# A recurrence's steps spread over a round of weight pieces, and an output projection whose last row blocks come after two columns

## The reference, cut to what matters

```python
def rglru(x, w_a, b_a, w_x, b_x, lam, reverse):
    r = sigmoid(einsum('bshc,hce->bshe', xh, w_a) + b_a)
    i = sigmoid(einsum('bshc,hce->bshe', xh, w_x) + b_x)
    log_a = -LRU_C * softplus(-lam) * r
    a = exp(log_a)
    u = sqrt(-expm1(2.0 * log_a)) * (i * x)
    _, h = lax.associative_scan(_recurrence_combine, (a, u), reverse=reverse, axis=1)
    return h

def recurrent_group(xr, gr, ...):
    xc = centred_depthwise_conv(xr, conv_w, conv_b)
    h = rglru(xc, ..., reverse=False) + rglru(xc, ..., reverse=True)
    return gelu(gr) * h
...
h = h + concatenate([a_out, b_out], axis=-1) @ w_out      # a_out: the recurrence, b_out: the gating
h = h + peer(rms_norm(h, ffn_norm_g), ...)
```

## Time and profile before

| | us |
|---|---|
| median of 3 runs | 3032.75 (3028.52 to 3043.32) |
| the profiled execution | 3043.12 |
| its span, first to last instruction | 3041.8 |
| TensorE busy in the span | 2912.6 (96%) |
| input projection of the second mixer in the span | 1254.3 to 1434.7 |
| second output projection | 1434.7 to 1528.5 |

### The profile page before, as it was taken

The page is one execution under the profiler, slowest core; times in us unless marked ns, Lnnn a source line. Parts: engine busy times, 40 slices in busy tenths (PEclk is TensorE's granted clock), DMA queues, the critical chain, the costliest instruction groups (busy, mean ns, idle before and its releaser), DMA issues.

```text
span 3041.8 us, 45087 instructions
## 1 busy us (share of the span) xinstructions
PE 2912.6 (96%) x18238; PEld 2622.7 (86%) x18238; DVE 2178.8 (72%) x3236; ACT 1594.5 (52%) x2418; POOL 412.5 (14%) x311
## 2 busy tenths in 40 slices
PE   7999989999999998988998899999999999999998
PEld 6888777888888886988888799999999999999997
DVE  5455457777776445554579899877999877999776
ACT  4477745555554444566444455544555544556543
POOL 0011100111111000242121000033110033100130
PEclk9999999999999999999999899999999999999999
DMA  6534354555555553633654455688766688666784
GB/s 239 180 139 141 136 194 146 186 184 189 183 191 215 193 192 139 223 138 133 222 181 153 168 192 181 224 313 314 246 234 232 222 317 314 237 231 228 279 308 165
DMA packets 99150, 631.42 MB, mean 208 GB/s; under 512 B 11520, under 2 KB 12928, under 8 KB 31360
## 3 DMA queue, kind: packets, MB, share of 16 engines
q1 hardware_dynamic: 80512, 561.43, 52.3%
q0 software_dynamic: 18432, 67.12, 6.1%
HBM read 623.26 MB, written 4.19 MB: 206 GB/s over the span
## 4 chain that ended last, share of the span: by engine, by line
PE 62%; DVE 10%; DMA 10%; ACT 3%; issue 1%; POOL 1%; ACTq 0%; DVEq 0%; POOLq 0%
PE ps L277 24%; PE ps L278 12%; PE ps L1260 5%; DMA ring<-in_u_rows_dram,idx 5%; DMA ring<-in_v_rows_dram,idx 5%; PE ps L299 4%; PE ps L300 4%; PE ps L301 4%; DVE loR L259 3%; PE ps L1262 3%; DVE ring L1321 1%; PE ps L1171 1%; PE ps L288 1%; PE ps L289 1%; PE ps L290 1%
## 5 line engine op out<-in xcount | busy, mean ns | idle before, releaser
L259 DVE TENSOR_TENSOR loR<-raw,hiR 128x1024 fp32r<-128x1024 f32 x1007 | 1266.1, 1264 | 600.8 <-ACT hiR L251 593.4
L251 ACT CAST hiR<-raw 128x1024 fp32r<-128x1024 f32 x1026 | 1073.7, 1049 | 715.1 <-PE ps L1262 320.2
L277 PE MATMUL ps<-XA,hiR 128*128 128x448 f32 (+1 forms) x3936 | 1355.5, 394 | 22.5 <-DVE S__142 L1203 22.0
L278 PE MATMUL ps<-XA,loR 128*128 128x224 f32 (+1 forms) x3936 | 1073.0, 273 | 0.0
L277 PEld LDWEIGHTS ps<-XA,hiR 128*128 128x128 f32 x3936 | 743.6, 189 | 140.5 <-DVE S__142 L1203 24.2
L278 PEld LDWEIGHTS ps<-XA,loR 128*128 128x128 f32 x3936 | 752.0, 191 | 2.5 <-issue 1.9
L1260 PE MATMUL ps<-hl,hiR 128*128 128x448 f32 x2048 | 648.8, 376 | 3.4 <-DVE loR L259 3.4
L1262 PE MATMUL ps<-hl,loR 128*128 128x224 f32 x2048 | 542.7, 265 | 0.0
L1260 PEld LDWEIGHTS ps<-hl,hiR 128*128 128x128 f32 x2048 | 384.4, 188 | 38.8 <-DVE loR L259 5.3
L1262 PEld LDWEIGHTS ps<-hl,loR 128*128 128x128 f32 x2048 | 391.4, 191 | 0.2 <-issue 0.2
L1299 POOL DMA_INDIRECT ring<-in_u_rows_dram,idx x64 | 103.2, 1613 | 727.8 <-DVE ring L1321 666.4
(11 more groups left out here) (284 smaller groups left out, 3473.1 us busy)
## 6 DMA issues: line engine op xcount, KB each, us to landing
raw<-in_u_dram SPq DMA_DIRECT2D x128, 1024.0 KB, 4.9
raw<-in_v_dram SPq DMA_DIRECT2D x128, 1024.0 KB, 5.7
raw<-in_w_up_dram SPq DMA_DIRECT2D x86, 1024.0 KB, 4.9
raw<-in_w_down_dram SPq DMA_DIRECT2D x43, 1024.0 KB, 4.9
raw<-in_w_in_qk_dram SPq DMA_DIRECT2D x32, 1024.0 KB, 4.9
raw<-in_w_out_dram SPq DMA_DIRECT2D x32, 1024.0 KB, 4.9
raw<-in_w_in_dram SPq DMA_DIRECT2D x24, 1024.0 KB, 4.9
raw<-in_w_in_v_dram SPq DMA_DIRECT2D x16, 1024.0 KB, 5.0
```

The costliest lines, as they stand in the source:

```text
L251: e.copy(hiR[:, r:r + 2, :], raw[n % NR][:, q:q + 2, :]).then_inc(S("hi"), 1)
L259: e.tensor_tensor(loR[:, r:r + 2, :], raw[n % NR][:, q:q + 2, :], hiR[:, r:r + 2, :].bitcast(F32), ALU.subtract).then_inc(S("lo_pool" if p ...
L277: e.matmul(both, wh, X.hl[:, :, k, 0:nt], start=(k == 0), stop=False, skip_group_check=True)
L278: m = e.matmul(dst[:, 0:nt], wl, X.h[:, k, 0:nt], start=False, stop=(k == KC - 1), skip_group_check=True)
```

## The change

Three things.

1. The chain of a round is spread over d = 25 to 42 in place of 23 to 32. Sigmoids: group 0 at 25, group 1 at 27. Tanh 29, gelu of `grT` 30, exp 31, square root 33. VectorE: 34, 35, and the scans at 36 and 38. Pool: products at 26 and 28, sums at 37 and 39, low parts at 40 and 42. High parts on ScalarE at 39 and 41. No operation is added or taken away.
2. In the input projection the pool makes no low parts any more; VectorE makes those eight pairs too.
3. The second output projection goes through columns 0 and 1 without row blocks 6 and 7, then (0, 6), (0, 7), (1, 6), (1, 7), then columns 2 and 3 as before. Column 0 is complete after 30 pieces and column 1 after 32 (before: 16 and 32), and `dve_x2` and the squares follow. The weights lie in HBM in the new order. SP's wait ahead of the four constant loads is for `gm_lo` and for `l_lo`, the recurrence's last low part.

```diff
-WO2_ORDER = [0, 1, 2, 3, 4, 5, 8, 9, 10, 11, 12, 13, 14, 15, 6, 7]
+MIX2 = [0, 1, 2, 3, 4, 5, 8, 9, 10, 11, 12, 13, 14, 15]
+WO2_ORDER = ([(0, k) for k in MIX2] + [(1, k) for k in MIX2] + [(0, 6), (0, 7), (1, 6), (1, 7)] +
+             [(2, k) for k in MIX2 + [6, 7]] + [(3, k) for k in MIX2 + [6, 7]])
+WO2_END = [30, 32, 48, 64]
...
-    if P_IN <= g < P_WO2:
-        return u % 6 == 0
...
-            if d == 23:
-                for i in range(2):
-                    c = 2 * p + i
...
-            elif d == 24:
+            if d in (25, 27):
+                i = (d - 25) // 2
+                c = 2 * p + i
...
+            elif d == 29:
...
-            if n % 16 == 0 and n:
-                dve_x2(e, n // 16 - 1)
+            if n in WO2_END:
+                dve_x2(e, WO2_END.index(n))
...
                 e.wait_ge(S("gm_lo"), 8)
+                e.wait_ge(S("l_lo"), 8)
```

More of the change, by code:

```diff
@@ L795, in act_mixer @@
             d = s - 24 * p
-            if d == 23:
-                for i in range(2):
-                    c = 2 * p + i
[L799 to L807, removed]
-            elif d == 24:
+            if d in (25, 27):
+                i = (d - 25) // 2
+                c = 2 * p + i
+                e.wait_ge(S("gates"), c + 1)
+                if p:
+                    e.wait_ge(S("hsum"), c - 1)
+                for v in range(2):
+                    e.activation(lR[i][:, v, :], bank[4 + 2 * i][:, v * T:(v + 1) * T], ACT.Sigmoid,
+                                 bias=lv[:, 40 + 8 * v + c:41 + 8 * v + c]).then_inc(S("sig"), 1)
+                for v in range(2):
+                    e.activation(lI[i][:, v, :], bank[5 + 2 * i][:, v * T:(v + 1) * T], ACT.Sigmoid,
+                                 bias=lv[:, 56 + 8 * v + c:57 + 8 * v + c]).then_inc(S("sig"), 1)
+            elif d == 29:
                 e.wait_ge(S("lam"), 24)
@@ L815, in act_mixer @@
                                      scale=lz[:, 80 + 8 * v + c:81 + 8 * v + c]).then_inc(S("tanh"), 1)
-            elif d == 25:
+            elif d == 30:
+                for i in range(2):
+                    c = 2 * p + i
+                    e.wait_ge(S("inev"), 6 * p + 2 + 2 * i)
+                    e.activation(grT[:, c, :], grT[:, c, :], ACT.Gelu_apprx_tanh).then_inc(S("grg"), 1)
+            elif d == 31:
                 for i in range(2):
@@ L823, in act_mixer @@
                                      scale=st[:, 200 + 8 * v + c:201 + 8 * v + c]).then_inc(S("aexp"), 1)
-            elif d == 26:
+            elif d == 33:
                 for i in range(2):
@@ L828, in act_mixer @@
                     e.activation(lR[i][:, :, :], lT[i][:, :, :], ACT.Sqrt, scale=-1.0).then_inc(S("lroot"), 1)
[L829 to L835, removed]
+            elif d in (39, 41):
+                c = 2 * p + (d - 39) // 2
                 e.wait_ge(S("hprod"), c + 1)
@@ L856, in dve_mixer @@
                                            lX[i][:, :], ALU.mult, ALU.add).then_inc(S("xc"), 1)
-            elif d == 26:
+            elif d == 34:
                 for i in range(2):
@@ L861, in dve_mixer @@
                                            ALU.mult).then_inc(S("q1"), 1)
-            elif d == 27:
+            elif d == 35:
                 for i in range(2):
@@ L866, in dve_mixer @@
                     e.tensor_tensor(lI[i][:, :, :], lI[i][:, :, :], lR[i][:, :, :], ALU.mult).then_inc(S("lu"), 1)
-            elif d in (28, 29):
-                i = d - 28
+            elif d in (36, 38):
+                i = (d - 36) // 2
                 e.wait_ge(S("lu"), 2 * p + i + 1)
@@ L888, in pool_mixer @@
             d = s - 24 * p
[L889 to L895, removed]
+            if d in (26, 28):
+                i = (d - 26) // 2
+                e.wait_ge(S("sig"), 8 * p + 4 * i + 4)
+                e.tensor_tensor(lI[i][:, :, :], lI[i][:, :, :], lX[i][:, None, :].to_broadcast([128, 2, T]),
+                                ALU.mult).then_inc(S("ix"), 1)
+            elif d in (37, 39):
+                i, c = (d - 37) // 2, 2 * p + (d - 37) // 2
                 e.wait_ge(S("scan"), 2 * c + 2)
@@ L900, in pool_mixer @@
                 e.tensor_tensor(lQ[i][:, 0, :], lQ[i][:, 0, :], grT[:, c, :], ALU.mult).then_inc(S("hprod"), 1)
-            elif d in (31, 32):
-                c = 2 * p + d - 31
+            elif d in (40, 42):
+                c = 2 * p + (d - 40) // 2
                 e.wait_ge(S("l_hi"), c + 1)
@@ L1464, in pe_program @@
                 pe_mixer(e, 4 * j + q)
-        for fb in range(4):
+        for n, (fb, k) in enumerate(WO2_ORDER):
             pair = (2 * (fb % 2), 2 * (fb % 2) + 1)
-            if fb == 0:
+            if n == 0:
                 e.wait_ge(S("inev"), 24)
-            elif fb >= 2:
+            elif (fb, k) == (1, 0):
+                e.wait_ge(S("gm_add"), 8)
+            elif fb >= 2 and k == 0:
                 e.wait_ge(S("x2"), 2 * (fb - 1))
[L1471 to L1478, removed]
+            e.wait_ge(S("l_lo" if k < 8 else "gm_lo"), k % 8 + 1)
+            moving(e, P_WO2 + n, XA.h[:, k, :], XA.l[:, k, :], [bank[b][:, :] for b in pair], k == 0, k == 7)
+            pe_mixer(e, 96 + n)
         for q in range(4):
@@ L1593, in act_program @@
             act_mixer(e, 96 + n)
-            if n % 16 == 1 and n > 16:
-                act_x2_square(e, n // 16 - 1)
+            if n - 1 in WO2_END:
+                act_x2_square(e, WO2_END.index(n - 1))
         act_x2_square(e, 3)
@@ L1754, in dve_x2 @@
     def dve_x2(e, fb):
-        e.wait_ge(S("piece"), P_WO2 + 16 * fb + 16)
+        e.wait_ge(S("piece"), P_WO2 + WO2_END[fb])
         for tb in range(2):
@@ L1965 @@
     a["w_in2"] = _stat(np.concatenate(blocks, 1))
-    a["w_out2"] = _mov(I["w_out_2"][0], [(fb, k) for fb in range(4) for k in WO2_ORDER])
+    a["w_out2"] = _mov(I["w_out_2"][0], WO2_ORDER)
     a["w_q"] = _stat(I["peer_w_q_2"][0])
```

## The result

| | us |
|---|---|
| before, median of 22 runs | 3037.99 (3028.52 to 3051.64) |
| changed, median of 22 runs | 3023.58 (3012.15 to 3037.67) |
| ratio | 0.9942, 95% interval 0.9930 to 0.9954 |
| profiled span | 3020.7 (before: 3041.8) |

A forecast was written before the change was run, and what follows sets the result against it. TensorE's single waits and the low clock behind them were taken to bound the kernel. The terms 11.3 + 4.4 + 3.6 - 1.0 - 0.5 = 17.8 us gave 3015 from the median 3032.75; range 3005 to 3029.

The forecast's parts named there:

- What bounds the kernel: Input and output projection: TensorE loses time in single waits and the low clock behind them, together 29 us.
- the ten waits: Input projection, rounds 1 to 3: TensorE waits for low parts from VectorE and the pool, costing 18.3 us, 6.1 a round.
- The walk: Step-by-step timing of one spread round from piece 24: waits at pieces 38, 40, 44 and 46, 2.35 us a round.
- The low clock: Input projection: four stretches at 1.2 GHz cost 5.8 us; one was expected to stay, so 4.4 us won.
- Rival (c): Input projection: spread waits keep TensorE at the low clock for long; with 20 such pieces 3044 us; chance 0.04.
- The border: Between the projections: `guT` comes ahead of the sigmoids, winning 3.6 us, 2.2 of wait and 1.4 of low clock.
- The output projection: Beside the last chain, early waits at pieces 14, 16 and 20 grow to about 2.5 from 1.5 us: -1.0 us.
- tile 8 and `x2`: Output projection, piece 32: tile 8 queued behind constant loads delays `x2`; none to 1.8 us of wait, taken as -0.5 us.
- The rest of the program is the same instructions in the same order: Outside the changed stages: claimed nothing differs, so no gain or loss was counted there.
- The rule of the shared port: VectorE with two SBUF inputs and the pool: the first takes the ports, the other blocks; a 1.22 us subtraction took 3.42.
- Rival (d): ScalarE's chain: a table switch costs 1.4 us more than its load, 5.5 us more wait a round; about 3037; chance 0.02.
- Rival (a): Both projections: stalls only move, all four low-clock stretches remain; 9.3 us won, 3023.5 us; chance 0.33.

The follow-up runs named there:

- part 2 alone: The kernel before with no low parts on the pool in the input projection, chain not spread: 173.4, 90.5 and 12.8 us; ratio to before 0.9964.

## Why the prediction was right, and where not

**What bounds the kernel** held, and so did the reading of the ten waits as 18.3 us. By this count the wait of the walk's check, at piece 30, is 0.91 + 0.16 = 1.07 us; the 1.19 in the text runs from the start of the matmul before. **The walk** named the three pieces that wait in every round. Its sizes were 0.55, 1.2 and 0.45 (with 0.15 at piece 46), 2.35 us a round; the trace has 0.63, 0.66 and 1.34, 2.63 us. The 1.2 was too large because the two products took 1.29 us together and not 1.75; the 1.8 of the earlier trace rows has a blocked part in it. The 0.45 was too small by the pool: I took 2.1 us for sum and product from the earlier trace rows, and they took 3.25, since VectorE's subtraction now stands right ahead of the sum. So the 11.3 of the sum is 10.4.

**The low clock** was 4.4 us of the sum, on the reading that one of four stretches stays. None did: 5.8 us. With the 10.4 that makes 16.2, and with the 2.4 at the border 18.6 for the stage. Rival (c), the low clock for longer, has nothing in this stage; but whether the clock falls can't be read from a single wait: the wait of 2.3 us at piece 32 brought no low stretch in the changed kernel and, 1.8 us long, one of 3.7 us in the kernel with the gelu moved:

```profile
1445.30:1449.00 3.70, 3.70 (x11) 2.88 (x10) 2.35 (x3) 1.81 (x4) 0.00 (x0) 0.54 0.61 257
```

**The border** was right: 2.86 us of wait became 0.47, and the low clock behind it is gone. Its 1.4 us can't be parted from the wait at piece 10, as the second trace of the kernel before shows; the sum holds all the same, since the walk gives what is left.

**The output projection is the term that failed.** The sum had -1.0 for its early waits and -0.5 for tile 8 and `x2`, and so 90.6 us for the stage; it took 93.6. The early ones came to 2.9 us in place of the forecast 2.5. A wait for `x2` at piece 32, which the prediction had among the signs of being wrong, came and cost 2.0 us more than the 0.5. The 0.6 us that is left has no term in the walk: the piece right behind a wait takes 1.45 to 1.49 us in place of 1.36, which makes up some 0.4 of it. Tile 8 was mis-sized, first by the time of its issue. `l_lo` 8 was there at 34.0 of the walk, not at 31.5. The pool had again stood behind VectorE: two low parts of 0.74 us took 3.44 together.

```profile
1434.28 3.44 POOL L906 TENSOR_TENSOR XA<-lQ,XA 128x256 fp32r<-128x256 f32 x2
```

The transfer took 9.9 us from its issue, close to the upper of the two values that I had (10.5, and 7.9 by the landing at 41.5; the text beside it says 7.7). It landed at 46.1, and the chain of 4.65 us from cast 32 to `x2` ended 2.5 us after piece 32 was wanted. The mechanism was in the text. The choice between its ends was wrong, and with `l_lo` 2.5 us later even the upper end, 1.8, was too low: it was 2.5 in place of 0.5.

**"The rest of the program is the same instructions in the same order"** was false by one: the norm behind the output projection has no table load. This gave 1.1 of the 1.6 us by which the third stretch is shorter (next section). The rest of it, 0.5 us, is within the 12.8 to 13.3 that the kernel before itself shows.

**The rule of the shared port** (Trainium skill, "SBUF — State Buffer", on the engine ports) was used in one direction only, for where the pool holds VectorE. The Trainium skill says that the first of the two takes the pair and the other blocks, whichever it is. The trace agrees in the other direction too: 0.74 us became 2.17 and 1.66 when VectorE had started 0.16 us earlier. Read so, it would have given the 3.25 us of sum and product, and with them the size of the wait at piece 44. In the last chain the same two blocks stand, 2.17 us for a sum and 3.44 for the low parts. That they account for most of the 2.5 us by which `l_lo`, and with it tile 8, came later than in the walk is an estimate: 1.4 and 2.0 us over the free times, on a path that isn't theirs alone.

**Rival (d)** is settled: in the changed kernel the four switches of a chain take 1.28 us each and the next function starts within 0.02 us of the load's end. The drain of 1.38 us that the Trainium skill ("ScalarE: Activation LUTs", on what a table load costs) adds isn't seen in these rows.

**Rival (a)** said 3023.5 us, and the median is 3023.6; this doesn't speak for it. It and the forecast's 3015 were set against 3032.75, the median of 3 runs, where the 22 runs of that kernel have 3038.0. What (a) says is a gain of 9.3 us, which lies outside the interval of the ratio (14 to 21 us) and far from the 17.1 us of the stretches. Of its terms, tile 8 was the right place and cost more than its 1.8, and its -1.2 for the early waits came to -1.4; but 3.2 us a round was 2.63, and of the four low stretches none stayed.

**All terms.** Forecast: 11.3 + 4.4 + 3.6 - 1.0 - 0.5 = 17.8. Measured, by the stretches: 10.4 + 5.8 + 3.8 - 1.4 - 2.5 - 0.6 for the pieces behind waits, + 1.6 for the norm = 17.1. The low clock, the norm and the border gave 3.2 us more than forecast, the rounds and the output projection cost 3.9 us more.

## What to carry to other kernels

When a burst on a side engine holds up a stream, spread it by the stream's own slack (ring depth times piece time, less cast and subtraction; an estimate that no run here tests), and then walk every engine that the burst passes: here ScalarE's list set the waits at pieces 38 and 40, the pool behind VectorE most of that at 44, the DMA queue that at piece 32 of the output projection, and each was taken away by an edit of its own. A late consumer order (part 3) is worth what it allows. Loads for the next stage, here two of 1 MB and two smaller ones, should not stand ahead of a tile that the present one needs within 10 us of its issue: it took 9.9.

## What the runs showed of the hardware

- For subtractions, sums and products with two inputs in SBUF, VectorE and the pool block each other, and which one pays goes by which started first. VectorE's subtraction of 1.22 us ran 3.42 us beside the pool, and the pool's sum of 0.74 us ran 2.17 us beside VectorE.
- A table load can vanish through an order far away. With the gelu ahead of the root, the root's table is still loaded when the norm behind the output projection takes its root. VectorE's reciprocal, first before and then changed:

```profile
1532.19 0.17 DVE L359 RECIPROCAL st<-st 128x2 f32<-128x2 f32 x1 [1.45 <-ACT st L355]
```

```profile
1501.01 0.17 DVE L361 RECIPROCAL st<-st 128x2 f32<-128x2 f32 x1 [0.36 <-ACT st L357]
```

  TensorE's wait for the norm is 3.66 us in all kernels with the table kept, and 4.75 with the load (before in both traces, part 2 alone, and the gelu behind the root in all rounds).
- The low clock repeats with the schedule within the input projection. Two traces of the kernel before have it behind the same waits there, at the same offsets to 0.1 us; at the start of the output projection one has it for 3.4 us and the other for 6.8. The kernel without the pool's low parts, with three waits of 2.1 us fewer, has one stretch in place of four.
